# Choosing the sparse half of the experts earlier, and moving a second modulation forward, in a two-block transformer kernel on one core

## What is computed

```python
mod = jnp.einsum('bd,de->be', c, w_mod[l]) + b_mod[l]     # block 1; block 2: silu(c_2) @ w_ada_2 + b_ada_2
q = (h @ w_query).reshape(B, S, 8, 2, 128)
sc = jnp.einsum('bshpc,hpnc->bshpn', q, sub_keys)
s1, i1 = lax.top_k(sc[..., 0, :], 16); s2, i2 = lax.top_k(sc[..., 1, :], 16)
top_s, sel = lax.top_k(cand_s, 16)            # of the 16 x 16 sums s1 + s2, with cand_i = i1 * 128 + i2
gates = jax.nn.softmax(top_s, axis=-1)
a = jax.nn.gelu(jnp.einsum('cd,chkd->chk', xc, expert_u[idx])) * gates
out = jnp.einsum('chk,chkd->cd', a, expert_v[idx])
```

## Time and profile before

| | us |
|---|---|
| median of three timed executions | 1991.19 |
| the profiled execution | 1992.43 |
| its span | 1990.6 |
| busy in the span: TensorE matmul | 1890.8 |
| busy: VectorE | 1618.9 |
| busy: ScalarE | 1080.0 |
| busy: GpSimd | 537.5 |

### The profile page before, as it was taken

How to read it: one execution, slowest core, us unless ns; L and a number is a source line. 1 busy time by engine, 2 the same in 40 slices (tenths; PEclk the granted TensorE clock), 3 DMA queues, 4 the chain that set the end, 5 groups by cost and what they waited for, 6 DMA issues and landing times.

```text
span 1990.6 us, 35711 instructions
## 1 busy us (share of the span) xinstructions
PE 1890.8 (95%) x13380; PEld 1835.2 (92%) x13380; DVE 1618.9 (81%) x3400; ACT 1080.0 (54%) x2111; POOL 537.5 (27%) x482
## 2 busy tenths in 40 slices
PE   7999999999999989999979998999999999999997
PEld 5998999999999988999979988899989999999997
DVE  3777658888899889999777775588788998899887
ACT  3455646634566555555555553465445665555554
POOL 0000003435433233444100000034344322534341
PEclk8999999999999999999989999999999999999999
DMA  9765556678799899999856772566787998999994
GB/s 351 271 222 175 182 184 213 223 267 283 266 316 310 312 370 363 382 334 348 321 189 205 255 251 76 164 212 223 262 279 264 319 318 292 348 353 356 341 352 166
DMA packets 143323, 543.30 MB, mean 273 GB/s; under 512 B 15728, under 2 KB 16112, under 8 KB 138288
## 3 DMA queue, kind: packets, MB, share of 16 engines
q1 hardware_dynamic: 99168, 362.86, 52.0%
q0 software_dynamic: 39456, 151.67, 21.2%
q10 hardware_dynamic: 4528, 26.49, 3.5%
HBM read 539.25 MB, written 1.05 MB: 271 GB/s over the span
## 4 chain that ended last, share of the span: by engine, by line
PE 60%; DMA 14%; DVE 14%; issue 6%; ACT 5%; POOL 1%; ACTq 0%; SPq 0%; DVEq 0%; POOLq 0%
PE PB L959 15%; PE PB L983 10%; DMA RING<-in_v 9%; DVE WL L1732 6%; PE PB L984 5%; PE PB L956 4%; PE PB L566 4%; PE PB L926 4%; PE PB L567 4%; PE PB L568 4%; DMA RING<-in_u 4%; ACT WH L1261 3%; PE PB L954 2%; PE PB L875 2%; DVE AR L1756 1%
## 5 line engine op out<-in xcount | busy, mean ns | idle before, releaser
L1732 DVE TENSOR_TENSOR WL<-RING,WH 128x1024 fp32r<-128x1024 f32 x517 | 634.7, 1230 | 213.9 <-ACT WH L1261 212.4
L1261 ACT ACTIVATE WH<-RING 128x1024 fp32r<-128x1024 f32 x517 | 545.2, 1056 | 403.9 <-DMA RING<-in_v 194.3
L983 PE MATMUL PB<-HX,WH 128*128 128x384 f32 x2048 | 595.5, 363 | 24.5 <-DVE WL L1732 18.6
L984 PE MATMUL PB<-HX,WL 128*128 128x192 f32 x2048 | 514.8, 251 | 0.0
L983 PEld LDWEIGHTS PB<-HX,WH 128*128 128x128 f32 x2048 | 385.4, 188 | 33.9 <-issue 33.0
L984 PEld LDWEIGHTS PB<-HX,WL 128*128 128x128 f32 x2048 | 392.8, 192 | 0.0
L959 PE MATMUL PB<-AR,RING 128*128 128x192 f32 x2144 | 376.5, 329 | 5.9 <-ACT AR L1534 5.8
L959 PEld LDWEIGHTS PB<-AR,RING 128*128 128x128 f32 x2144 | 351.8, 192 | 6.6 <-ACT AR L1534 6.3
L2481 POOL DMA_INDIRECT AR<-in_v,SPX x128 | 239.2, 1869 | 350.3 <-DVE AR L2205 294.3
L956 PE MATMUL PB<-HX,WH 128*128 128x384 f32 x854 | 254.4, 362 | 0.0
L954 PE MATMUL PB<-HX,WL 128*128 128x192 f32 x976 | 228.2, 254 | 0.0
(11 more groups left out here) (267 smaller groups left out, 2861.1 us busy)
## 6 DMA issues: line engine op xcount, KB each, us to landing
RING<-in_u SPq DMA_DIRECT2D x256, 512.0 KB, 5.0
RING<-in_v SPq DMA_DIRECT2D x256, 512.0 KB, 6.4
RING<-in_win SPq DMA_DIRECT2D x90, 512.0 KB, 4.6
AR<-in_wr ACTq DMA_DIRECT2D x20, 1024.0 KB, 7.3
RING<-in_wq SPq DMA_DIRECT2D x32, 512.0 KB, 3.6
AR<-in_wr POOLq DMA_DIRECT2D x16, 1024.0 KB, 5.2
AR<-in_wm SPq DMA_DIRECT2D x8, 1024.0 KB, 16.1
RING<-in_wout SPq DMA_DIRECT2D x16, 512.0 KB, 5.4
```

The source lines that it names most:

```text
L983: e.matmul(both_parts(c), hi(n_v + n)[:, cs], dense(k), start=start, stop=False)
L984: return e.matmul(PB[c][:, 0:T], lo(n_v + n)[:, cs], HH[:, k, 0:T], start=False, stop=stop)
L1261: e.activation(hi(t), raw(("w", t), words(t)), ACT.Copy).then_inc(s_hi, 1)
L1732: e.tensor_tensor(lo(t), raw(("w", t), words(t)), hi(t).bitcast(F32), ALU.subtract).then_inc(s_lo, 1)
```

## The change

The modulation chunks 24 to 31 (the first 8 of block 2) leave the down tiles of block 1. GpSimd now fetches them once the mixing ahead of block 1's output projection is done, into the space of two tensors that are dead by then; VectorE sums four of them in the output projection and four in the query projection. The condition vector gets a copy of its own (CRX), fetched by SyncE and put through Silu by ScalarE before the output projection.

Of the choice, the half with the sparse tokens is now spread over the first 30 tiles and the other half over tiles 30 to 81; the second key scores stand before tile 22. There are 72 unsplit tiles: 12 of the first 30 (where j % 5 is 1 or 3), every third from 34 to 64, and 32, 68, 73 and 78, beside those from 83 on. The first 16 dots are at tiles 35 to 65 and the other 48 at tiles 83 to 118; ScalarE's gelu of the dots moves from the third down tile to up tile 119, and 10 of the 64 sums follow beside tiles 120 to 127. The remaining 54 are spread over the down tiles.

ScalarE activates a split tile two tiles later instead of one, and an unsplit one at the start of the next step; TensorE waits for a split tile's PSUM bank only until its product has been read, and no longer for the gelu. GpSimd's partial product is kept three tiles ahead of its place rather than one.

```diff
-EARLY = 12
+EARLY, DOTS_END, SUMS_BESIDE = 16, 118, 10
 for _m in range(GK):
-    DOT_AT.setdefault(46 + 2 * _m if _m < EARLY else JG - 1 + (_m - EARLY) * (NK - JG + 1) // (GK - EARLY), []).append(_m)
-for _m in range(GK, N_GATHER):
-    SUM_AT.setdefault(4 + (_m - GK) * 119 // GK, []).append(_m)
-GELU_AT = 2
+    DOT_AT.setdefault(35 + 2 * _m if _m < EARLY else JG - 1 + (_m - EARLY) * (DOTS_END - JG + 2) // (GK - EARLY), []).append(_m)
+for _m in range(SUMS_BESIDE):
+    DOT_AT.setdefault(DOTS_END + 2 + _m * (NK - DOTS_END - 2) // SUMS_BESIDE, []).append(GK + _m)
+for _m in range(GK + SUMS_BESIDE, N_GATHER):
+    SUM_AT.setdefault(2 + (_m - GK - SUMS_BESIDE) * 121 // (GK - SUMS_BESIDE), []).append(_m)
+GELU_AT = DOTS_END + 1
-RAW = [j >= JG - 1 or j in (5, 12, 19, 26, 33, 40) or j in range(45, 69, 2) or j in (71, 74, 77, 80) for j in range(NK)]
+RAW = [j >= JG - 1 or (j < HALF and j % 5 in (1, 3)) or j in range(34, 66, 3) or j in (32, 68, 73, 78) for j in range(NK)]
...
-        share, count = sum(work) * min(j + 1, JG - 2) / (JG - 2), 0
+        share, count = sum(CHOICE) * (min(j + 1, HALF) / HALF + max(0, min(j + 1, JG - 2) - HALF) / (JG - 2 - HALF)), 0
...
+                if (kind, i) == ("w", W_VV):
+                    e.wait_ge(s_zp, 5)
+                    e.dma_start(CRX, cr2).then_inc(s_crx, 16)
...
                     if j >= 3:
-                        e.wait_ge(s_act, NK * blk + j - 2)
+                        if RAW[j - 3]:
+                            e.wait_ge(s_act, NK * blk + j - 2)
+                        elif POOL_ADDS[j - 3]:
+                            e.wait_ge(s_part, parted(blk, j - 3))
+                        else:
+                            e.wait_ge(s_sum, added(blk, j - 3))
...
+            e.wait_ge(s_crx, 16)
+            e.activation(CRX, CRX, ACT.Silu).then_inc(s_silu, 1)
             sqrt_table()
...
                     fill(n_u + j)
-                    if j and WIDE[j - 1]:
-                        e.wait_ge(s_sump if POOL_ADDS[j - 1] else s_sum, added(blk, j - 1))
-                        e.activation(PG[:, j - 1, :], PG[:, j - 1, :], gelu).then_inc(s_act, 1)
+                    if j == GELU_AT:
+                        e.wait_ge(s_spent, N_GATHER * blk + GK)
+                        e.activation(GEL[:, :], DOT[:, :], gelu).then_inc(s_gel, 1)
+                    if 2 <= j < JG and WIDE[j - 2]:
+                        summed(j - 2)
+                    if 1 <= j < JG and RAW[j - 1]:
+                        unsplit(j - 1)
+                    if j == JG - 1 and WIDE[j - 1]:
+                        summed(j - 1)
...
             for i, (c, u) in enumerate(OUT_ORDER):
                 fill(W_OUT + i)
+                if 3 <= i < 7:
+                    row_sum(21 + i, 0)
+                    row_sum(21 + i, 1)
...
+                            if blk == 0 and t in (7, 9, 11, 13):
+                                row_sum(28 + (t - 7) // 2, 0)
+                                row_sum(28 + (t - 7) // 2, 1)
...
-                    if blk == 0:
-                        chunk_step(n)
...
-                            e.tensor_tensor(PG[:, j, :], PG[:, j, :], PG[:, j + 1, :], ALU.add).then_inc(s_sump, 1)
+                            e.tensor_tensor(PG[:, j, :], PG[:, j, :], PG[:, j + 3, :], ALU.add).then_inc(s_sump, 1)
...
+            e.wait_ge(s_y, 8)
+            for g in range(24, 24 + N_EARLY):
+                if g >= 26:
+                    e.wait_ge(s_mdv, g - 25)
+                e.dma_start(row_chunk(g), row_source(g)).then_inc(chunk_landed(g)[0], 16)
             peer(0, ur1, v1)
```

More of the change, by code:

```diff
@@ L23 @@
 JG = 84
+HALF = 30
+SCORES = 22
 SP = 64
@@ L76 @@
 ROW_LAND = {g: sum(ROW_SLOT[h] == s for h in ROW_SLOT if h <= g) for g, s in ROW_SLOT.items()}
-V_FIRST = 12
-N_IN_V = 8
+N_EARLY = 8
 N_MID = 8
-IN_V = {V_FIRST + 8 * i + 4 * (i > 0): 24 + i for i in range(N_IN_V)}
 OUT_ORDER = [(0, 0), (1, 0), (0, 1), (1, 1), (2, 0), (2, 1), (3, 0), (3, 1)]
@@ L361, in two_block_kernel @@
         GATE2 = ar(1024, 4, 2, 4, 256)
-        ROWS1, ROWS2, ROWS3 = ar(26112, 3, 2, D), [ar(28672, 2, D), ar(30720, 2, D)], ar(7680, 2, 2, D)
+        ROWS1, ROWS2, ROWS3 = ar(26112, 3, 2, D), ar(9216, 2, 2, D), ar(7680, 2, 2, D)
+        CRX = ar(15360, D)
         MR0, MR4 = ar(19232, N_START, 256), ar(13312, 4, 256)
@@ L1521, in stage, with summed, unsplit @@
                     e.activation(HH[:, n % 4, 0:T], PG[:, V_ORDER[n], :], ACT.Copy).then_inc(s_ah, 1)
+                def summed(t):
+                    e.wait_ge(s_sump if POOL_ADDS[t] else s_sum, added(blk, t))
+                    e.activation(PG[:, t, :], PG[:, t, :], gelu).then_inc(s_act, 1)
+                def unsplit(t):
+                    e.wait_ge(s_used, n_u + t + 1)
+                    e.activation(PG[:, t, :], PB[1 + (8 + t) % 3][:, 0:T], gelu).then_inc(s_act, 1)
                 for j in range(NK):
@@ L1574, in peer @@
                     fill(n_v + n)
[L1575 to L1582, removed]
+                    if blk == 0 and n == 12:
                         e.wait_ge(s_cr, 32)
                         e.activation(CR[1], CR[1], ACT.Silu).then_inc(s_silu, 1)
-                    if n == GELU_AT:
-                        e.wait_ge(s_spent, N_GATHER * blk + GK)
-                        e.activation(GEL[:, :], DOT[:, :], gelu).then_inc(s_gel, 1)
                     if n == SQRT_AT:
@@ L1753, in row_sum @@
                     e.wait_ge(s_cr, 16)
-                if (g, j) == (24, 0):
-                    e.wait_ge(s_silu, 1)
-                r = e.tensor_tensor_reduce(w, w, CR[g // 24], 1.0, 0.0, ALU.mult, ALU.add, MC[:, c:c + 1])
+                if (g, j) in ((24, 0), (24 + N_EARLY, 0)):
+                    e.wait_ge(s_silu, 1 if g == 24 else 2)
+                by = CRX if 24 <= g < 24 + N_EARLY else CR[g // 24]
+                r = e.tensor_tensor_reduce(w, w, by, 1.0, 0.0, ALU.mult, ALU.add, MC[:, c:c + 1])
                 if j:
@@ L2250, in peer @@
                     fill(n_v + n)
-                    if blk == 0:
-                        chunk_step(n)
-                        if IN_V.get(n - 4) == 23 + N_IN_V:
-                            e.wait_ge(s_mdv, N_IN_V)
-                            add_rows(48, 48 + 2 * N_IN_V, C_B2, 2)
+                    if blk == 0 and n == 12:
+                        e.wait_ge(s_mdv, N_EARLY)
+                        add_rows(48, 48 + 2 * N_EARLY, C_B2, 2)
                     for m in SUM_AT.get(n, ()):
@@ L2534, in peer @@
                 gathers(N_GATHER)
+            e.wait_ge(s_y, 8)
[3 more added lines that the diff above has]
+                e.dma_start(row_chunk(g), row_source(g)).then_inc(chunk_landed(g)[0], 16)
             peer(0, ur1, v1)
-            for g in range(24 + N_IN_V, 48):
-                if g < 24 + N_IN_V + N_MID:
-                    e.wait_ge(s_mdv, max(N_IN_V, g - 25))
+            for g in range(24 + N_EARLY, 48):
+                if g < 24 + N_EARLY + N_MID:
+                    e.wait_ge(s_mdv, max(N_EARLY, g - 25))
                 else:
```

39 lines of the change are left out of this document (19 added, 20 removed).

## The result

The changed kernel takes 2048.26 us (median of 4 runs, 2045.73 to 2056.54), the kernel before 1991.81 beside it (1985.76 to 1997.19). The ratio is 1.0282, 95% interval [1.0244, 1.032]. The prediction, 1979 and at most 2006, was wrong in sign and size.

A forecast was written before the change was run, and what follows sets the result against it. TensorE, busy for 95% of the span, was taken as the bound. From the profiled 1992.4 us, -18.3 - 4 + 7 - 6.6 + 10 = -11.9 gave 1980.5; with the median 1.2 lower, 1979 us, range 1956 to 2006.

The forecast's parts named there:

- Tiles 83 to 127: +5 us in each block: Tiles beside the gates: 48 dots instead of 41 cost VectorE and gather time, +5 us a block, bounds 0 and +26.
- Rival A: Gates: the gathers pace them, from a landing of 6.6 us on; +18 instead of +5 a block, 2005 us; chance 0.21.
- Up tiles 0 to 82: -3.3 in each block: Early up tiles: 1.6 - 5.5 + 2 - 1.4 = -3.3 us a block, bounds -10 and +14.
- What could be worse is the ring: Up tiles beside early dots: split tiles four after unsplit ones come late; +2 us taken, +21 if all are late.
- The handover: Up tiles 42 to 45: later activation covers TensorE's wait behind GpSimd's add and the slow restart, -5.5 us a block.
- rival D: Handover not mended: ScalarE's queue still stops at the add, +5.5 us a block, 1990 us; chance 0.24 together with B.
- No change: Up tiles: VectorE has room for a half of the choice in 30 tiles, 90% busy in both halves, no cost.
- +1.6 for the unsplit tiles: Up tiles 0 to 82: 27 unsplit and 56 split tiles instead of 22 and 61 cost TensorE +1.6 us.
- The down tiles: -22: Down tiles: without the chunks block 1 comes down to block 2, -18.3 us; fewer sums give -2 in each block.
- The -2 for the sums: Down tiles: the 10 sums leaving each block give -2 us in each, bounds 0 to -5.
- The front of block 1: +7: Front of block 1: chunks summed there delay the norm, +6 us, and the query projection, +1; upper bound 14.
- rival B: Chunks no cheaper in front: half of the 18 us stays, the front costs 14, 1996 us; chance 0.24 together with D.

The follow-up runs named there:

- e2: Changed kernel with the 67 unsplit tiles of the kernel before in place of 72 (4 of the first 30 instead of 12): 2020.31 us, ratio 1.0136.
- e8: Changed kernel, still 72 unsplit tiles, but 1, 3, 21 and 23 split and 71, 76, 80 and 81 unsplit instead: 2030.21 us, ratio 1.0174.
- e3: Kernel before with the later activation alone, TensorE waiting only for the read of PSUM, partial product three tiles ahead: 1980.87 us, ratio 0.9943.
- e5: Changed kernel with u gathers of 256 instead of 1024 columns, VectorE's work unchanged, sparse part of the result left out: 2006.49 us, ratio 1.0083.
- e9: e7 with the choice's first half spread over the first 30 up tiles and second key scores at tile 22: 1993.7 us, ratio 1.0007.
- e4: Kernel before with the modulation in front alone (eight chunks, CRX and the row sums): 1989.62 us, ratio 0.9978.
- e1: Changed kernel with the last 48 dots spread over tiles 83 to 126 and no sums beside the gates: 2016.64 us, ratio 1.010.
- e7: Kernel before with the later activation and the modulation in front together: 1979.61 us (10 runs), ratio 0.9946.

## Why the prediction was wrong, step by step

**"Tiles 83 to 127: +5 us in each block"** is the first step that failed: it came out at +20.0 and +13.3, and at 9.5 to 16.1 in e2 and e8. The bounds were right, and so was the mechanism named for the upper one. The value between them was wrong, and so was its sum. I wrote 6.3 us to landing and 1.3 for dot and issue, 7.6 for three gathers, against 7.9 wanted. The gathers start 3.11 us apart, 9.3 for three (in block 2 2.92, 8.8 for three). From a gather's start to a dot that waited for it the trace has 6.1 us at least, 7.5 in the median and 9.1 at most (19 dots of block 1); the dot itself is 1.2, and the buffer is free only at its end, so 8.7 in the median, plus what GpSimd still has in hand. I had taken the median landing of a stretch in which most gathers weren't waited for. The rows could have said so: 41 dots in 126.2 us are 3.08 apart, and VectorE already waited 5.4 us for gathers at that pace. The supply had little left there: asked for one in 2.63, it gave one in 2.9 to 3.1, in e2 and e8 too. Rival A's condition, a landing above 6.6 us, held, and its +18 is near the mean of after's two blocks, 16.7.

**"Up tiles 0 to 82: -3.3 in each block"** is the second, and the larger: it came out at +18.3 and +14.9. I take each tile's time from its start to the next one's start, less 2.60 or 2.28 us, and 3.5 for the scores. Its terms, block 1 and block 2:
- *"What could be worse is the ring", +2*: this is the term that failed. In the first 30 tiles it is +14.5 in both blocks, 3.4 to 3.5 us at tiles 2 and 3 and 11 at tiles 21 to 26. I had looked for it only beside the early dots and had not put the score tiles into the ring's order, which take two of four slots just behind two unsplit tiles. The stop is then long enough for the clock to fall: 0.94 granted, 1.00 in e8. Beside the early dots, tiles 30 to 82 take 7.9 and 3.5 us more than in e3 without its scores, some 3 of the 7.9 by the handover below; e5 takes 8.0 and 4.0 back. That both parts together, 18 to 20, come near my bound of 21 is luck: the bound was for eleven pairs beside the early dots, where only 3.5 to 5 lie. I had dropped it because "most split tiles are fetched ahead", and around the scores they can't be.
- *The handover, -5.5, and -1.4 for other activations*: right on the kernel before. e3 has -6.8 and -6.6 in tiles 30 to 82. But of my sign, no pause at tiles 31 to 34 either, a part failed in the changed kernel. In block 1 its tiles 34 and 35 take 4.6 and 3.8 us:

```profile
413.45 0.60 POOL L2510 TENSOR_TENSOR AR<-AR 128x192 f32<-128x192 f32 x1
414.08 0.36 ACT L1540 ACTIVATE AR<-AR 128x192 f32<-128x192 f32 x1 [3.99 <-POOL AR L2510]
414.35 0.31 ACT L1544 ACTIVATE AR<-PB 128x192 f32<-128x192 f32 x1
...
414.71 0.44 PE L966 MATMUL PB<-HX,WH 128*128 128x384 f32 x1 [1.86 <-ACT AR L1544]
```

  GpSimd again issues three gathers before the add, and ScalarE's queue again stops at it, as rival D had it. Tile 32 is unsplit now, so TensorE must wait before tile 35 for its activation, which stands behind that add; the release by the reading of PSUM is for split tiles alone. In block 2 these tiles take 2.5 and 2.7, without the pause.
- *"No change" for the half in 30 tiles*: held within 1.1 and 1.9 us, what the other tiles of the first 30 take more than before. It holds only for the 18 splits that I had counted: with 26 it is +7.0 (e9). My comparison didn't show it either. By the same prices the two halves before come to 90 and 93%, not 92 and 91, and the first 30 tiles before, which are what the new ones replace, to 88% (61.84 of 70.60 us). And a mean share says nothing of two splits with 2 us of choice between them; which split is late is what counts. e5 shows the opposite case, 127.29 of 129.10 us busy and nothing late.
- *+1.6 for the unsplit tiles*: stands by count, 0.32 each.

The terms add up: 1.6 - 6.8 + 14.5 + 7.9 + 1.1 = 18.3.

**"The down tiles: -22"**: -12.8 and +0.4 instead of -20.3 and -2. The mechanism held, since the same 12.8 went in e4, where nothing else was changed. The -2 for the sums isn't seen; e1 put them back, and the blocks moved by +2.3 and -1.0. The two blocks are 5.1 us apart, not within the 3 of my sign, and block 1 is under its 308. In block 1 TensorE is *busy* 303.41 us for the 2072 matmuls that take 297.54 in block 2. So the 5.9 us between them are not idle time at all. The trace shows how. From the first line to the last of each of these two pieces sixteen pairs of matmuls (lines 996 and 997) start, in block 1 and then in block 2:

```profile
849.81 0.37 PE L996 MATMUL PB<-HX,WH 128*128 128x384 f32 x1
...
854.45 0.37 PE L996 MATMUL PB<-HX,WH 128*128 128x384 f32 x1
```

```profile
1769.78 0.36 PE L996 MATMUL PB<-HX,WH 128*128 128x384 f32 x1
...
1774.33 0.36 PE L996 MATMUL PB<-HX,WH 128*128 128x384 f32 x1
```

They take 4.64 and 4.55 us, at a granted clock of 1.00 in both places, which makes 2.32 and 2.28 us a tile. Nearly all tiles 8 to 119 of block 1 are of the first kind and most of block 2 of the second, so this is some 4.5 of the 5.9. The rest is about what short spells at the lower clock make: with one digit more than the view has, the trace's clock is 0.989 and 0.995 over the two stretches. e2's block 1 runs at 2.32 too, e7's at 2.28 for the most part; they lie at 303.8 and 300.0. What sets the one pace or the other stays open.

**"The front of block 1: +7"**: +11.5. I counted VectorE's delay of the norm. The changed kernel's waits from 217.5 to 308.1 show it, and the timeline where it ends:

```profile
PEld PB L640 <- DVE AR L1758: 6.8, 1, 6.8
```

```profile
249.09 3.67 PE L640 MATMUL PB<-KC,AR 128*128 128x128 f32 x16 [6.29 <-DVE AR L1758]
252.56 3.41 PE L613 MATMUL PB<-KC,AR 128*128 128x1 f32 x16
```

The output projection and what follows it up to this wait end 2.0 us later than before, and the wait is 6.3: 8.3 where I had 6. VectorE's own wait for a chunk (in_wr) is only 1.3 us of it. What I left out is what follows. The same two groups of matmuls took 1.97 and 1.85 us before; now they run at about half the pace, and the slow spell reaches into the first 48 of the query projection, 8.6 us instead of 7.7. The granted clock is 0.88 in the stretch to 253.0 and 0.92 in the next. That restart makes 3.2 us, net of a pause of 0.8 before the queries that is gone, and 8.3 + 3.2 are the 11.5. The 14 of my upper bound had it; the 7 had not, with its +1 for the queries. (The 55.10 us from 253.0 and the 49.10 before, from 247.5, aren't the same work: the query projection starts 2.8 us behind the one bound and 2.3 ahead of the other.)

Most of the signs that I had named did their work: the pause at tiles 44 and 45 is gone, though one came at 34 and 35 in block 1; the waits for gathers are 20.8 and 14.3 us; VectorE's splits release TensorE's idle time. I had said that I would be wrong as a whole if the gates stretch beyond 172 us: they take 185.0 and 178.2. A small slip besides: rival B's 1996 adds 8 for a front that costs 14 instead of 7; it is 1995.

## What to carry to other kernels

Where a consumer waits now and then for transfers with few buffers, take the pace seen for the supply's limit, and divide the stretch by the count before you ask for more: three buffers gave one 512 KB gather in 3.1 us here before, and 2.9 to 3.1 when one in 2.6 was asked for. A ring slot is held until its last reader, so a change in which tiles are split is a change in when slots come free: list the holders of every slot, the odd tiles too, around the tightest place. A share of 90% on an engine that feeds the bound one is not room; ask which single instruction comes too late when a block of other work is put before it. And when one part of a change relieves what another loads, as the unsplit tiles did for VectorE, the cost of a part alone (e9) is not its cost in the whole.

## What the runs showed of the hardware

GpSimd's adds and VectorE's passes over two operands in SBUF slow each other, which I hadn't counted in the early tiles. The adds of the candidates in e9 (duration ns min/median/max) and VectorE while eight of them run (380.23 to 389.70):

```profile
L2543 POOL TENSOR_TENSOR AR<-AR x16: 728/1196/1730, 365.5 to 389.0; 128x256 f32<-128x256 f32 x16
```

```profile
380.07 1.22 DVE L1751 TENSOR_TENSOR WL<-RING,WH 128x1024 fp32r<-128x1024 f32 x1
381.20 1.76 DVE L2114 TENSOR_TENSOR AR<-AR,KC 128x1024 f32<-128x1024 f32 x1
382.89 1.76 DVE L1751 TENSOR_TENSOR WL<-RING,WH 128x1024 fp32r<-128x1024 f32 x1
```

The same add takes from 0.73 to 1.73 us and the same split 1.22 or 1.76. The page "SBUF — State Buffer" of the Trainium skill (SBUF: two separate sides) has a VectorE instruction with two SBUF inputs and a GpSimd instruction that reads SBUF exclude each other for a whole instruction; these rows agree with it. What share of e9's 7.0 us comes of this was not tried.

The other surprise is the one left open above: the same 16 pairs of matmuls take 4.55 or 4.64 us at the same granted clock of 1.00, and keep to one pace over a hundred tiles.
